# Layer 1's first branch: two evictions moved ahead of the gates' chain, and one unit's low weight parts moved from VectorE to GpSimd

## The reference

```python
h = rmsnorm(x, norm_w) * (1.0 + scale) + shift
aq, ak, av, ag, ao, az, bq, ... = split_cols(h @ w_in)
# first branch: a scan with input and forget gates, 4 heads, both directions
pre = ag + b_if                       # gates
fwd = (pre[0], jax.nn.log_sigmoid(pre[1]))
bwd = (pre[2], jax.nn.log_sigmoid(pre[3]))
b = cumsum(fc); dmat = where(tril, b_t - b_s + i_s, -inf)
m_row = maximum(max(dmat), inter)     # running maxima
a = exp(dmat - m_row) * (q @ k^T)     # then a @ v, divided by its row sum
y_a = rmsnorm(h_a) * sigmoid(o) * silu(z)
```

## Time and profile before

| | |
|---|---|
| median of 3 runs | 2453.19 us (2451.3 to 2456.11) |
| the profiled execution, its own time | 2449.05 us |
| its span | 2447.3 us |
| PE busy | 2318.2 us (95%) |
| DVE busy | 1293.4 us (53%) |
| ACT busy | 1036.4 us (42%) |
| POOL busy | 249.6 us (10%) |
| mean granted TensorE clock | 0.986 of full speed |

### The profile page before, as it was taken

One profiled execution on the slowest core, in us unless ns is written; L12 is line 12 of the kernel. 1 busy time (PEld: TensorE's weight loads), 2 busy tenths in 40 slices (PEclk: granted clock), 3 DMA queues, 4 the chain that ended last, 5 costly groups with the idle time before them and its releaser, 6 DMA issues.

```text
span 2447.3 us, 38568 instructions
## 1 busy us (share of the span) xinstructions
PE 2318.2 (95%) x16336; PEld 2099.0 (86%) x16336; DVE 1293.4 (53%) x2505; ACT 1036.4 (42%) x1987; POOL 249.6 (10%) x252
## 2 busy tenths in 40 slices
PE   5999999999999999899999999998988999998998
PEld 3788878989868988789899889998788999878998
DVE  5544423567543223564556664366655555665654
ACT  2433322444532232344434454453555444465443
POOL 0100001222101021000013220210100110100110
PEclk9999999999999999999999999999999999999999
DMA  6321134211234212222242223355223545413544
GB/s 238 108 85 70 52 140 164 77 70 63 76 121 148 77 70 97 84 104 102 105 155 87 89 95 142 125 192 175 102 110 114 183 170 176 142 53 111 183 169 142
DMA packets 50411, 291.45 MB, mean 119 GB/s; under 512 B 8960, under 2 KB 13312, under 8 KB 19072
## 3 DMA queue, kind: packets, MB, share of 16 engines
q1 hardware_dynamic: 50240, 289.00, 32.6%
HBM read 286.89 MB, written 2.36 MB: 118 GB/s over the span
## 4 chain that ended last, share of the span: by engine, by line
PE 80%; DVE 12%; ACT 6%; issue 1%; DMA 1%; POOL 0%; DVEq 0%; SPq 0%; ACTq 0%; POOLq 0%
PE PS L520 77%; DVE wl L1943 3%; PE PS L524 2%; DVE wl L1945 2%; ACT TM L1371 2%; ACT TMG L1371 2%; ACT wh L1381 1%; DVE TM L1924 1%; DVE HYl L1932 1%; DVE TM L1932 1%; DVE colS L1932 1%; DVE TMG L1932 1%; DVE colS L2250 1%; DMA X<-in_xin 0%; ACT HYh L1371 0%
## 5 line engine op out<-in xcount | busy, mean ns | idle before, releaser
L520 PE MATMUL PS<-HYh,wh 128*128 128x256 f32 (+1 forms) x3000 | 949.5, 316 | 35.7 <-DVE HYl L1932 14.6
L520 PE MATMUL PS<-HYl,wh 128*128 128x256 f32 (+1 forms) x3000 | 934.6, 312 | 0.0
L520 PE MATMUL PS<-HYh,wl 128*128 128x256 f32 (+1 forms) x3000 | 934.4, 311 | 0.0
L1943 DVE TENSOR_TENSOR wl<-raw,wh 128x1280 fp32r<-128x1280 f32 (+2 forms) x254 | 371.9, 1464 | 549.3 <-ACT wh L1381 549.2
L520 PEld LDWEIGHTS PS<-HYh,wh 128*128 128x128 f32 x3000 | 575.5, 192 | 78.4 <-DVE HYl L1932 16.6
L520 PEld LDWEIGHTS PS<-HYh,wl 128*128 128x128 f32 x3000 | 575.4, 192 | 30.6
L520 PEld LDWEIGHTS PS<-HYl,wh 128*128 128x128 f32 x3000 | 576.1, 192 | 29.0
L1381 ACT ACTIVATE wh<-raw 128x1280 fp32r<-128x1280 f32 (+2 forms) x254 | 306.8, 1208 | 329.0 <-PE PS L520 251.4
L520 PE MATMUL PS<-wh,HYh 128*128 128x256 f32 x1458 | 425.1, 292 | 17.9 <-DVE HYl L1932 6.8
L520 PE MATMUL PS<-wl,HYh 128*128 128x256 f32 x1458 | 415.8, 285 | 0.0
L520 PE MATMUL PS<-wh,HYl 128*128 128x256 f32 x1458 | 415.7, 285 | 0.0
(11 more groups left out here) (178 smaller groups left out, 1764.1 us busy)
## 6 DMA issues: line engine op xcount, KB each, us to landing
raw<-in_wpk SPq DMA_DIRECT2D x235, 1024.0 KB, 4.8
raw<-in_wpk SPq DMA_DIRECT2D x32, 704.0 KB, 4.1
TM<-in_wpk SPq DMA_DIRECT2D x4, 1024.0 KB, 18.3
X<-in_xin SPq DMA_DIRECT2D x1, 2048.0 KB, 10.1
Y<-in_wpk SPq DMA_DIRECT2D x2, 1024.0 KB, 23.9
Y<-bias_d SPq DMA_DIRECT2D x4, 512.0 KB, 10.1
raw<-in_wpk SPq DMA_DIRECT2D x3, 512.0 KB, 3.6
T<-in_tabs SPq DMA_DIRECT2D x1, 1216.0 KB, 14.7
```

What stands on the lines that cost most here:

```text
L520: return P.x.matmul(o, l, r, start=start, stop=stop)
L1943: D.x.tensor_tensor(wl[:, s, 0:c], raw[:, r, 0:c], wh[:, s, 0:c], ALU.subtract).then_inc(*lo_split.mark())
```

## The change

Three things are done.

1. In `branch_a` of ACT, for layer 1 only, `qk(0)`, the two evictions of the first head's queries and keys, stands right behind the conversion of the unit a_v and ahead of the gates' eviction and its Abs, Exp and Ln. The conversion of the unit a_o (`used("a_qk", 4 * l)`) stays behind the chain.
2. The low part of the unit (a_qk, 4), which is layer 1's a_qk unit of the first head, is made by GpSimd (`low_weights`), after its last work of layer 0, instead of by DVE between `rstd(1)` and `modulated1()`. It is the same subtraction in the same two pieces.
3. What waited for DVE's count of this unit waits for GpSimd's step instead: PE ahead of the unit's first matmul, SP ahead of the load into the same raw slot (that of a_o).

```diff
+    lows_by_pool = [place["a_qk", 4]]
...
             def weights(u):
-                P.wait_ge(lo_split, u)
+                if u in lows_by_pool:
+                    P.wait_ge(pool_step, ("low", u))
+                else:
+                    P.wait_ge(lo_split, u)
...
                 if l:
                     used("gate", l)
+                    qk(0)
                 act(a_gt, bank(2), ACT.Identity, ("a_gt", l), bias=vcol(f"bif{l}"))
...
-                qk(0)
+                if l == 0:
+                    qk(0)
+                used("a_qk", 4 * l)
                 v_half(0, 0)
...
                     rstd(1)
-                    used("w_out", 3)
                     modulated1()
...
+            def low_weights(u):
+                n, c, s, r = words[u], cut_of(u), slot(u), u % NRAW
+                for i, (a, z) in enumerate(((0, c), (c, n))):
+                    G.wait_ge(hi_split, (u, i))
+                    tt(wl[:, s, a:z], raw[:, r, a:z], wh[:, s, a:z], ALU.subtract, ("low", u))
...
                 merge(l, "c")
+                if l == 0:
+                    low_weights(lows_by_pool[0])
...
-                    if units[b][1] == "conv":
+                    if b in lows_by_pool:
+                        S.wait_ge(pool_step, ("low", b))
+                    elif units[b][1] == "conv":
                         S.wait_ge(lo_split, b)
```

More of the change, by code:

```diff
@@ L1394, in branch_a, with qk @@
                 t0, N = lay(l)
+                def qk(h):
+                    A.wait_ge(projected, ("a_q", l, h))
+                    act(a_qk[:, 0, t0:512], bank(0)[:, 0:N], ACT.Copy, ("a_q", l, h))
+                    A.wait_ge(projected, ("a_k", l, h))
+                    act(a_qk[:, 1], bank(1), ACT.Copy, ("a_k", l, h), scale=128.0 ** -0.5)
                 A.wait_ge(projected, ("gate", l))
@@ L1408, in branch_a @@
                 act(a_g[:, 0], a_g[:, 0], ACT.Ln, ("a_ln", l), bias=1.0)
[L1410 to L1415, removed]
                 def v_half(h, b):
@@ L1477, in branch_a @@
                         qk(h + 1)
+                        used("a_qk", 4 * l + h + 1)
                         v_half(h + 1, 0)
```

## The result

The changed kernel is slower. In 8 runs its median was 2459.3 us (2457.68 to 2463.16), that of the kernel before 2452.28 us in the 8 runs beside them; the ratio is 1.0026 with a 95% interval of 1.0017 to 1.0036, or 6.4 us (4.2 to 8.8). The forecast was 2458.7 us, 5.5 us more than the 2453.19 us then on record. The profiled execution took 2460.25 us, its span 2458.4.

A forecast was written before the change was run, and what follows sets the result against it. PE was taken as the bound, busy 95% of the span, so time moves only where PE waits. Terms 3.97 - 0.03 - 0.4 + 2.0 = 5.5 us on 2453.19 gave 2458.7 us, range 2453.6 to 2461.2.

The forecast's parts named there:

- The low part leaves DVE: Ahead of layer 1's modulated1: DVE no longer making a_qk's low part gains 0.03 us on the path, not 2.27.
- GpSimd holds the root: DVE's inverse root before layer 1: GpSimd's two pieces hold its second and fourth instructions, ending it 3.97 us later.
- The evictions: ACT, layer 1: values start 3.7 us earlier, but the gates' chain lets only 0.4 us arrive at o_gate(0).
- The clock: PE at the start of o_gate(0): after the new waits it falls to its lower level, costing 2.0 us.
- The sum: All terms together: 3.97 - 0.03 - 0.4 + 2.0 = 5.5 us slower.
- no hold: Rival at DVE's root: its small instructions aren't delayed by GpSimd; +1.6 us, 2454.8 us; chance 0.12.
- only the first piece: Rival at DVE's root: GpSimd's second piece delays nothing; term 2.5 us, sum 4.1, 2457.3 us; chance 0.08.
- a slow GpSimd: Rival at the low part: 4.7 ns a column, root 8.8 us late, sum 10.4, 2463.6 us; chance 0.06.
- faster: Rival behind the values: DVE's gates' chain is not the bound, PE keeps 5.6 us, 2447.6 us; chance 0.04.

The follow-up runs named there:

- e5: Kernel before, plus two GpSimd subtractions on unneeded data beside the root, DVE still making the low part; ratio to the kernel before 1.0011.
- e1: Changed kernel with the two evictions back behind the gates' chain, only the low part on GpSimd; ratio to the kernel before 1.0004.
- e3: Changed kernel, but GpSimd begins the low part only when DVE has ended the root; ratio to the kernel before 1.0006.
- e2: Changed kernel with the low part made by DVE again, only the evictions moved up; ratio to the kernel before 1.0008.
- e7: e6 plus, in layer 1, o_gate(0) ahead of the transposes and a_o's low part between DVE's scans; ratio to the kernel before 0.9978.
- e8: e2 plus unused PE matmuls, 15 behind the values and 6 behind the transposes; ratio to the kernel before 1.0004.
- e6: Kernel before, with ACT evicting the queries between Abs and Exp and the keys behind Ln; ratio to the kernel before 1.0004.
- e9: Kernel before with only, in layer 1, o_gate(0) ahead of the transposes and a_o's low part between DVE's scans; ratio 1.0000.
- e10: e2 plus, in layer 1, o_gate(0) ahead of the transposes and a_o's low part between DVE's scans; ratio to the kernel before 0.9999.
- e4: e2 plus 15 unused PE matmuls behind the values, ahead of the transposes; ratio to the kernel before 1.0015.

## Why the prediction came out right, step by step

**The low part leaves DVE: nothing.** Right. The spread was as long as DVE's work beside it, and e5, in which both engines do their part, is as late as e1.

**GpSimd holds the root: 3.97 us.** Right in mechanism, 3.76 us in size. GpSimd took 4.64 us for the two pieces, not 4.81, and held the second and the fourth instruction, not the third, which reads PSUM. e3 and e5 show that it is the overlap: moved behind the root, the same work costs 0.69 us; with other data, it costs the same. The Trainium skill, "SBUF — State Buffer", section "SBUF: two separate sides", says that the instruction that starts first has the pair of ports shared by GpSimd and DVE to its end, also against a DVE instruction with two inputs in SBUF. By that rule, these rows agree: the instructions held have both inputs in SBUF, and those with one in PSUM pass (0.16 us in the root, 1.28 us in e3).

**The evictions: 0.4 us earlier at `o_gate(0)`.** Right: 0.3 us, counted from the end of the keys' matmuls (18.97 us before, 18.68 now), and 0.46 us in e2. The wait did move from ahead of the values to behind them, onto the gates' chain: the gates' eviction starts 1.73 us later against the keys' matmuls, as forecast. e7 shows the other side: where that chain doesn't hold PE up and the clock stays at 1.00, the stage is 6.2 us shorter.

**The clock: 2.0 us.** The mechanism was right, the size somewhat large. From the start of `o_gate(0)` to the first pick PE took 7.41 us against 5.95, which is 1.46 us; e8 against e2 gives 1.70, and e6 2.2. The fall came earlier than forecast, in the wait for `a_rc`: part of the stretch at the lower clock passed over a wait and over the transposes. Their 0.60 us more shortened the wait for a_o, which DVE ends (1.02 us where about 1.5 were forecast), and cost nothing. Of the lower clock only what falls on matmuls that nothing else holds up is paid. What the forecast had not counted is that the clock also changed in the first units of layer 1: from their start to the end of the keys PE took 16.14 us instead of 16.63, which is 0.49 us back. By the trace's clock records the lower level stood over the first 5.2 us of them before and the first 4.1 us now.

**The sum.** 3.76 - 0.49 - 0.29 + 1.46 = 4.4 us in the stage, of 5.5 forecast. The path and the signs were right, but that the forecast of 5.5 us lies so near the measured 6.4 and 5.6 us is in part luck: its terms are 1.1 us too large in sum, and the 1 to 2 us by which the whole exceeds the stage were in none of them. Those are within the intervals, and whether they are a cost behind the stage is left open. The rivals are out: no hold (2.6 us rows), only the first piece (1.53 us at the fourth instruction), a slow GpSimd (4.64 us), and faster.

## What to carry to other kernels

Work moved to GpSimd to free DVE isn't free where it starts ahead of a chain of small DVE instructions: ask not how busy GpSimd is, but which DVE instructions with two SBUF operands stand beside it in time and who waits for them. Where a wait is taken away from the front of a stage, find the next event that ends it before counting the gain, and count what the clock does at the new wait. A gain can need a whole row of waits taken out together: e2, e6 and e9 each gave nothing alone, and e6 and e9 together gave 5.4 us (e7). Which two it is matters: e2 and e9 together gave nothing in the timed runs (e10).

## What the runs showed of the hardware that was not expected

The length of a wait alone didn't say whether the clock falls behind it. In the profile before, PE stood for 2.3 us at 1219 and went on at 1.00, and the forecast used this as a wait that the clock survives. The same wait, 2.25 or 2.26 us at the same place of the program, is in all thirteen profiles. The clock stayed at 1.00 behind it in six (before, e1, e5, e6, e8, e9) and fell in seven (the changed kernel twice, e2, e3, e4, e7, e10). The stretch behind it in the changed kernel:

```profile
1227.70:1231.40 3.70, 3.70 (x21) 3.70 (x22) 2.26 (x4) 1.33 (x3) 0.00 (x0) 0.60 0.00 0
```

The clock also fell behind shorter waits: 1.55 us in e4, with the 16 transposes of 4 rows (0.93 us) in front, and 0.99 us in e10, with matmuls of 4 rows in front again, whereas 0.36 us at the same place in e7 and 0.64 us behind full matmuls in e10 left it at 1.00. No run here varied these matmuls alone, so whether it is they that make the difference is open, and so is how far e4 against e8 would come out the same in another execution. In all four profiles that have the wait of 3.7 to 3.8 us for `a_rc` (the changed kernel twice, e2, e3) the clock fell in it.
